# Two transformer blocks on one core: the overfull check moved up, low parts of weights split behind the first columns, and PE's unread products taken out of norms and routing and put at the start

## The reference, cut to what matters

```python
def reference(x, ...):                      # x: 256 tokens x 1024, float32
    x = first_block(x, ...)                 # 2 layers
    return second_block(x, ...)             # 2 layers

def first_block(...):
    h = x
    for i in range(2):
        mix = gla_mixer(h, ...) if i == 0 else mlstm_mixer(h, ...)
        h = layer_norm(ALPHA * h + mix, ln_g[i, 0], ln_b[i, 0])
        ffn = grouped_moe(h, router_w, moe_w1[i], moe_w3[i], moe_w2[i])
        h = layer_norm(ALPHA * h + ffn, ln_g[i, 1], ln_b[i, 1])
    return h

def grouped_moe(x, w_router, w1, w3, w2):   # 16 experts, 2 of them for each token
    aff = sigmoid(t @ w_router)             # the best group of 4 experts, the best 2 in it
    for e in range(16):
        y += gates[:, e:e + 1] * ((silu(t @ w1[e]) * (t @ w3[e])) @ w2[e])

def second_block(...):
    for l in range(2):
        h = rms(x, g_mix[l]) * (1.0 + sc1) + sh1
        parts = split(h @ w_in[l])          # attention over 256 keys and dilated attention
        ...
        x = x + gt1 * (mixed @ w_out[l])
        h2 = rms(x, g_mlp[l]) * (1.0 + sc2) + sh2
        x = x + gt2 * (square(relu(h2 @ w_ff1[l])) @ w_ff2[l])
```

## Time and profile before

| | us |
|---|---|
| median of three runs | 1489.74 |
| the profiled execution, its own time | 1487.12 |
| its span, first to last instruction | 1485.3 |
| PE busy | 1437.2 (97%) |
| PE weight loads busy | 1068.0 (72%) |
| DVE busy | 913.1 (61%) |
| ACT busy | 626.4 (42%) |
| POOL busy | 39.5 (3%) |

### The profile page before, as it was taken

The page is one execution under the profiler, slowest core; times in us unless marked ns, Lnnn a source line. Parts: engine busy times, 40 slices in busy tenths (PEclk is TensorE's granted clock), DMA queues, the critical chain, the costliest instruction groups (busy, mean ns, idle before and its releaser), DMA issues.

```text
span 1485.3 us, 20562 instructions
## 1 busy us (share of the span) xinstructions
PE 1437.2 (97%) x8426; PEld 1068.0 (72%) x8426; DVE 913.1 (61%) x1549; ACT 626.4 (42%) x1004; POOL 39.5 (3%) x39
## 2 busy tenths in 40 slices
PE   7999999989999999999799999999999999999998
PEld 7885444436888634443578997999977898899997
DVE  4986111117787711111799987998969976775555
ACT  6453211115344221211455655454456566465443
POOL 0000000000000000000120000000002000000000
PEclk9999999999999999999999999999999999999999
DMA  9897999998467899999565463899955533445540
GB/s 373 316 362 299 426 426 427 427 425 334 153 248 309 320 422 427 426 427 425 230 238 195 174 247 146 322 367 360 347 196 185 198 118 123 158 170 191 180 169 29
DMA packets 59063, 420.18 MB, mean 283 GB/s; under 512 B 6657, under 2 KB 6721, under 8 KB 8658
## 3 DMA queue, kind: packets, MB, share of 16 engines
q1 hardware_dynamic: 58322, 417.17, 71.3%
q0 software_dynamic: 640, 1.61, 0.3%
HBM read 417.71 MB, written 1.05 MB: 282 GB/s over the span
## 4 chain that ended last, share of the span: by engine, by line
PE 81%; DVE 11%; DMA 4%; ACT 3%; issue 1%; SPq 0%; DVEq 0%; ACTq 0%
PE ps L867 78%; DVE lo L2098 2%; DMA AR<-in_moe 2%; DMA raw<-in_moe 2%; DVE AR L2091 2%; PE ps L1505 1%; DVE AR L2088 1%; DVE TINY L2091 1%; ACT AR L1997 1%; PE ps L1476 1%; PE ps L1232 1%; DVE ACC L2091 0%; ACT T L1665 0%; PE ps L983 0%; DVE AR L2737 0%
## 5 line engine op out<-in xcount | busy, mean ns | idle before, releaser
L2098 DVE TENSOR_TENSOR lo<-raw,hi 128x1024 fp32r<-128x1024 f32 x296 | 359.7, 1239 | 96.5 <-ACT hi L1647 95.8
L1647 ACT ACTIVATE hi<-raw 128x1024 fp32r<-128x1024 f32 x296 | 306.0, 1056 | 182.5 <-PE ps L867 177.2
L867 PE MATMUL ps<-T,hi 128*128 128x256 f32 x1792 | 325.3, 284 | 8.4 <-ACT hi L1647 7.4
L867 PEld LDWEIGHTS ps<-T,hi 128*128 128x128 f32 x1792 | 278.6, 191 | 16.5 <-ACT hi L1647 7.4
L867 PE MATMUL ps<-hi,T 128*128 128x512 f32 x896 | 286.1, 394 | 3.5 <-ACT T L1665 3.2
L867 PE MATMUL ps<-T,lo 128*128 128x256 f32 x896 | 249.3, 281 | 0.0
L867 PEld LDWEIGHTS ps<-hi,T 128*128 128x128 f32 x896 | 168.2, 188 | 40.4 <-ACT T L1665 3.9
L867 PE MATMUL ps<-lo,T 128*128 128x512 f32 x448 | 174.5, 390 | 0.0
L867 PEld LDWEIGHTS ps<-T,lo 128*128 128x128 f32 x896 | 169.5, 190 | 0.0
L867 PE MATMUL ps<-hi,AF 128*128 128x512 f32 x512 | 163.3, 390 | 0.0
L2091 DVE SCALAR_TENSOR_TENSOR AR<-AR,ps 128x512 f32<-128x512 f32 x52 | 35.4, 685 | 189.4 <-PE ps L867 102.3
(11 more groups left out here) (247 smaller groups left out, 1730.7 us busy)
## 6 DMA issues: line engine op xcount, KB each, us to landing
raw<-in_moe SPq DMA_DIRECT2D x76, 1024.0 KB, 17.4
raw<-in_b_ff SPq DMA_DIRECT2D x64, 1024.0 KB, 5.0
AR<-in_moe SPq DMA_DIRECT2D x59, 1024.0 KB, 17.1
raw<-in_ada SPq DMA_DIRECT2D x48, 1024.0 KB, 6.6
ring<-in_moe SPq DMA_DIRECT2D x45, 1024.0 KB, 16.0
raw<-in_b_in SPq DMA_DIRECT2D x24, 1024.0 KB, 5.8
raw<-in_b_gate SPq DMA_DIRECT2D x16, 1024.0 KB, 4.7
ACC<-in_moe SPq DMA_DIRECT2D x12, 1024.0 KB, 20.3
```

The lines of the kernel that those rows point to most:

```text
L867: return e.matmul(o, l, r, start=a, stop=z, skip_group_check=True)
L1647: e.activation(hi[n % NC][:, :], raw[place[c]][:, 1024 * half:1024 * half + 1024], ACT.Copy).then_inc(*to("hi", "hi", n))
L2098: tt(lo[n % NC][:, :], r, hi[n % NC][:, :], SUB).then_inc(*to("lo", "lo", n))
```

## The change

It has four parts. (1) The check for overfull experts stands behind pair 7's second up product (s = 1, after the maps) in place of behind its first down product; SP's check stands 12 chunks from the layer's end in place of 6; the waits of the full computation name what is last there. (2) `turned_columns` hands out one low part behind the high part of columns 0 and one behind that of columns 2, for all norms; the single low parts ahead of the columns in `walk_ln` and `walk_rms`, and the one between `layer_norm(3)` and the first rms norm, are gone. In the first rms norm the gain is computed ahead of the scale. Where a first product used to wait for both parts of its unit, it now waits for the high one, and the products with the low part stand behind; the kernel's very first block is cut in two halves of four blocks of columns. (3) All `fill` calls in norms and routing are gone. (4) At the start PE runs 8 unread products on zeros that POOL has set.

```diff
-def turned_columns(kind, feed, late):
+def turned_columns(kind, feed):
     for g in range(4):
         yield (kind + "_turn", g)
         if g:
             yield (kind + "_split", g - 1)
         yield (kind + "_hi", g)
-        if g == 2:
-            yield from feed.some_late(late)
+        if g % 2 == 0:
+            yield from feed.some_late(1)
     yield (kind + "_split", 3)
...
     yield ("ln_rows",)
-    yield from feed.some_late(1)
-    yield from turned_columns("ln", feed, 1)
+    yield from turned_columns("ln", feed)
     yield from feed.some_late(NC)
...
     yield ("sum_up", key)
-    yield ("fill", 16)
     yield ("rows", 0, 0)
...
     yield ("x_lo", 0, 0)
-    yield ("fill", 5)
     yield ("places",)
...
         if p < 8 and s == (1 if p else 3):
             yield ("maps", p)
+        if p == 7 and s == 1:
+            yield ("overflow",)
...
-        if p == 7 and s == 4:
-            yield ("overflow",)
...
     yield from (("sum_turn", k) for k in sums)
+    if first:
+        yield ("rms_gain",)
     yield ("rms",)
     yield from (("sum_out", k) for k in sums)
-    yield ("rms_gain",)
-    yield from feed.some_late(1)
-    yield from turned_columns("rms", feed, 0)
+    if not first:
+        yield ("rms_gain",)
+    yield from turned_columns("rms", feed)
...
                     w.wait_ge(*after("hi", n0))
-                    for k in range(kt):
-                        if k % 2 == 0:
-                            w.wait_ge(*after(*xs[k // 2]))
-                        mm(o, hi[n0][:, 128 * k:128 * k + 128], th[:, k, :], k == 0, False)
-                        mm(o, hi[n0][:, 128 * k:128 * k + 128], tl[:, k, :], False, False)
-                    w.wait_ge(*after("lo", n0))
-                    for k in range(kt):
-                        ins = mm(o, lo[n0][:, 128 * k:128 * k + 128], th[:, k, :], False, k == kt - 1)
+                    for ks in (range(4), range(4, 8)):
+                        for k in ks:
+                            if k % 2 == 0:
+                                w.wait_ge(*after(*xs[k // 2]))
+                            mm(o, hi[n0][:, 128 * k:128 * k + 128], th[:, k, :], k == 0, False)
+                            mm(o, hi[n0][:, 128 * k:128 * k + 128], tl[:, k, :], False, False)
+                        w.wait_ge(*after("lo", n0))
+                        for k in ks:
+                            ins = mm(o, lo[n0][:, 128 * k:128 * k + 128], th[:, k, :], False, k == kt - 1)
...
                     w.wait_ge(*after(xs[0][0].replace("split", "hi"), *xs[0][1:]))
                     for t in range(2):
                         for k in range(2):
                             mm(PS[bank[name, 0, t]][:, :], th[:, k, 128 * t:128 * t + 128], h[:, HALF[k]], k == 0, False)
+                    w.wait_ge(*after("lo", n0))
+                    for t in range(2):
+                        for k in range(2):
                             mm(PS[bank[name, 0, t]][:, :], th[:, k, 128 * t:128 * t + 128], l[:, HALF[k]], False, False)
...
                     if what == "ln_turn":
-                        if a[0] == 0:
-                            fill(30)
                         turn_columns("ln", LN_XN, a[0], q)
...
+                p = take("fill")
+                w.wait_ge(*after("zeros"))
+                for _ in range(8):
+                    mm(p[0:64, 0:256], m.KM[:, 0, 0, 64:128], m.KM[:, 0, 0, 64:128].unsqueeze(1).broadcast_to([128, 4, 64]), True, True)
+                free.append(bank["fill",])
...
                     elif what == "rms_turn":
-                        if a[0] == 0 and blk == 2:
-                            fill(10)
-                        elif a[0] == 0 and l == 0:
-                            fill(24, ("x", 3, 0, 1))
                         turn_columns("rms", src, a[0], l, blk)
...
-            first_of = {c0 - 6: i for c0, i in stops.items()}
+            first_of = {c0 - 12: i for c0, i in stops.items()}
```

More of the change, by code:

```diff
@@ L669, in two_block_kernel @@
         XLO = sb("XLO", [128, 2, 1024], F32R)
+        XL1 = XLO[:, :, :].rearrange("p t d -> p (t d)")
         ACC = sb("ACC", [128, 2048])
@@ L940, in block_b @@
                 got = []
-                for u in us:
-                    got.append(unit(u))
                 if n == 0 and gs[0] == 0 and xs[0][0] in ("ln_split", "rms_split"):
-                    (h, l), = got
+                    n0 = plan.units[us[0]][2]
+                    h, l = hi[n0 % NC], lo[n0 % NC]
+                    w.wait_ge(*after("hi", n0))
                     w.wait_ge(*after(xs[0][0].replace("split", "hi"), *xs[0][1:]))
@@ L956, in block_b @@
                     return
+                for u in us:
+                    got.append(unit(u))
                 for t in range(2):
@@ L1014, in sum_turn @@
                 give(("sum_turn", key), "sum_out", key)
-            def fill(n, *ready):
-                p = take("fill")
-                for x in ready:
-                    w.wait_ge(*after(*x))
-                for _ in range(n):
-                    mm(p[:, 0:256], IDR[:, :], XLO[:, 0, 0:256], True, True)
-                free.append(bank["fill",])
             def layer_norm(q, turned):
@@ L1167, in moe @@
                         give(("logits", i), "logits_out", i)
-                    elif what == "fill":
-                        p = take("fill")
-                        for _ in range(a[0]):
-                            mm(p[:, 0:256], IDR[:, :], T2[:, 2048:2304], True, True)
-                        free.append(bank["fill",])
                     elif what == "count":
@@ L1286, in full_tensor @@
                 v.wait_ge(*after("f_x", i))
-                v.wait_ge(*after("turned", i, 7))
-                v.wait_ge(*after("y_lo", i, 6, 0))
+                v.wait_ge(*after("silu", i, 7))
+                v.wait_ge(*after("map", i, 7))
+                v.wait_ge(*after("gain", i, 7))
+                v.wait_ge(*after("y_lo", i, 5, 1))
+                v.wait_ge(*after("turned", i, 6))
                 for k in range(8):
@@ L1622, in tensor_program @@
             layer_norm(3, False)
-            feed.some_late(1)
             for l in range(2):
@@ L1856, in full_scalar @@
                 spare = [bank["spare", i, x] for x in range(4)] if not rehearsing[0] else range(4)
-                v.wait_ge(*after("down", i, 6, 0))
+                v.wait_ge(*after("up", i, 7, 0, 1))
                 for k in range(8):
@@ L2872, in vector_program @@
             layer_norm(3, False)
-            for what, *a in feed.some_late(1):
-                common(what, a)
             for l in range(2):
```

## The result

The changed kernel is slower by 0.27%: its time over that of the kernel before is 1.0027, with a 95% interval of 1.0019 to 1.0035. The medians of 13 runs each are 1493.3 and 1489.6 us. 1493.3 lies inside the forecast's wide range (1485.5 to 1495) and just outside the range of its likeliest case (1487 to 1493). The forecast had called "same within 0.2%" the likeliest, with 0.59; what came is "slower", which had 0.25.

A forecast was written before the change was run, and what follows sets the result against it. PE, with 81% of the chain, was taken as the bound through its idle time and clock, DMA second in moe. Terms summed to +1.0 us on 1487.1, so 1488.1, or 1490.2 on the timed level; range 1485.5 to 1495.

The forecast's parts named there:

- wide range: Whole kernel: range of the time over all cases, 1485.5 to 1495 us.
- likeliest case: Whole kernel: the forecast itself, 1490.2 us on the timed level, own range 1487 to 1493, chance 0.50.
- Start: Kernel's start: 8 products on zeros let the first real products run at full clock; -1.0 us (-1.4 to 0).
- Routing: Routing of both layers: without fills the clock falls for some 3.3 us; +1.0 each, +2.0 us (0 to +3.4).
- Check of layer 0: Layer 0's overflow check, moved earlier: DMA holds the next products back in turn; -0.2 us (-0.8 to 0).
- Check of layer 1: Layer 1's overflow check, moved earlier: PE catches up with DMA, last product starts sooner; -1.3 us (-1.5 to -0.8).
- `ln1`: Norm `ln1`: 4.8 us idle, transposes at half clock use up the new order's gain; +0.6 us (-1.0 to +2.7).
- First rms norm: First rms norm: cold transposes, but first product no longer held by gain and low part; -0.4 us (-1.3 to +1.7).
- The two rms norms: Rms norms ahead of feed forward: idle grows to about 2.6 us, clock may fall; +0.65 each, +1.3 us (0 to +3.4).
- Faster without any fall of the clock: Rival for routing and rms norms: without fills the clock doesn't fall; sum -3.9, 1485.3 us; chance 0.18.
- Slower, since the clock comes back only with real products: Rival at the norms: transposes don't raise the clock, first products run low; +5.9 more, 1496 us; chance 0.25.
- The start does nothing: Rival at the start: small load late or zero products run into 7.43; +1.0 more, 1491.2 us; chance 0.07.

The follow-up runs named there:

- experiment 5: Changed kernel with all unread products of norms and routing put back and the check, SP's too, in its old place; 1.0018 to the kernel before.
- experiment 2: Changed kernel with the unread products of routing alone put back (16 and 5 in each layer); 0.9989 to the kernel before.
- experiment 4: Kernel before with its unread products taken out and nothing else changed; 1.0052 to the kernel before, +7.7 us.
- experiment 6: Kernel before with the 8 products on zeros at the start added, nothing else changed; 1.0015 to the kernel before, slower by 2.2 us.
- experiment 7: Kernel before with only the low parts' new order; products, check and start as before; 0.9999 to the kernel before.
- experiment 10: Kernel before with 12 products on a constant added in `mlstm`, nothing else changed; 1.0002 to the kernel before.
- experiment 9: Changed kernel with 12 products on a constant added in a wait in `mlstm`, moving later code; 1.0016 to the kernel before.
- experiment 1: Changed kernel with all unread products of norms and routing put back, the rest of the change kept; 0.9980 to the kernel before.
- experiment 12: Changed kernel with all unread products put back, but the 24 ahead of the first rms norm as 24 transposes of a constant; 1485.1 us (one run).
- experiment 3: Changed kernel with the unread products of the norms alone put back (30, 24, 10 and 10); 1.0001 to the kernel before.
- experiment 8: Changed kernel with 4 in place of 8 products at the start, 16 PE instructions fewer; 1497.8 us (one run).

## Why the prediction was right or wrong, step by step

The wide range held the time, and the bounding reasons were right: PE's waits and its clock set the time, the products lay in idle time, and what they did was to hold the clock. The likeliest case came out wrong by the sizes of its losses, and by one wait that it didn't have.

**Start: right in this execution.** -1.0 forecast, -0.98 in the ledger. In two of the other nine traces with products at the start the clock fell at 20 us and took 2.2 and 3.5 us back (experiments 5 and 2). And the same 8 products also moved all later code of PE by 32 instructions, which no step of the prediction looked at.

**Routing: mechanism right, size wrong.** Forecast +1.0 a layer "for a stretch like the 3.3 us of 701.20 to 704.50". Measured +1.8 and +2.2, with the clock low for 6.8 us in each. The one stretch that I had was taken for the length of them all; the other in the earlier trace rows, 6.7 us, would have given the right size.

**Check of layer 0: -0.2 forecast, -0.5 in the ledger, more in most executions.** Here the profiled execution of the kernel before misled me. It is the only one of six kernels with the check in the old place whose clock did not fall there (it did in experiments 4, 5, 6, 7 and 10). That the medians differ by 2 us less than the two profiles fits a fall of this kind in most executions of the kernel before. The mean granted clocks bear it out: the profiled execution has 0.997, and of the 78 timed beside the experiments 64 have 0.992 to 0.995. One more stretch of 6.8 us at 0.50 in 1485 makes 0.997 into 0.994. The 64 have a median of 1489.4 us and the other 14 one of 1488.0. So the forecast was made from one of the few lucky executions; where the clock fell in the others is not on record.

**Check of layer 1: wrong in its result.** Forecast -1.3, measured -0.1. The earlier check did what was hoped for: 1.49 us idle, no fall of the clock. In experiment 9, which has no second wait, the difference to the kernel before is +4.0 us at the end of routing and +1.8 behind the check, a gain of 2.2. The second wait of 2.79 us took it back. What the earlier place gives is a shorter idle time: in all 14 checks of the seven other kernels that have it there, and in both of the changed kernel, it was 1.3 to 1.8 us, against 2.3 to 3.6 in the 12 of the six kernels with the old place. In 11 of these 12 the clock fell, at the check or, in two, behind the second wait. Why it is shorter is seen in the loads of PE's code, in the last section.

**`ln1`: size wrong.** Forecast +0.6, if the clock was back soon after 350. The first product came at 350.66, as forecast (350.8), but the clock came back only at 353.4 and took the rest: +1.5. The sign that the forecast named for this (0.50 for over 5 us behind the transposes) came only if it is counted from their start: 6.1 us, against 2.4 from their end. And of the order's gain, for which the bounds had 1.0, experiments 1 and 7 show 0.3 left at the block's end, as the low part is then waited for.

**First rms norm: right**, -0.4 forecast, -0.6 measured together with `ln3`. The clock was low for 13.7 us, of which only 6 had work.

**The two rms norms: half right.** Forecast +0.65 each; measured +0.4 with 3.4 us at 0.50, and +2.0 with 6.8. As with routing, the length of the stretch decides.

**The rivals.** *Faster without any fall of the clock* is excluded by the windows. *Slower, since the clock comes back only with real products* named the side that came, for a reason that did not: experiment 12 has it back during transposes, and `ln1` and the first rms norm did not lose over 2 us each against the forecast. The Trainium skill, "TensorE: Matmul & The Clock Gate", Part 4 (PE-mode transpose), has it that the full clock doesn't engage for transposes. For getting it back the trace of experiment 12 disagrees: 0.50 until 723.4, 1.00 behind it, and no product from the first transpose (720.58) to 728.74. For keeping it the traces are divided. The forecast had one stretch of transposes alone at 1.00, from 1106.5 to 1111.7. In 11 of the 14 traces it is so; in three (experiments 3, 8 and 10), none of which changes anything there, the clock fell in it, as in experiment 3:

```profile
1110.63 3.01 PE L999 MATMUL ps<-cst,AR 128*128 128x128 f32 x16 [1.35 <-DVE AR L2095]
```

*The start does nothing* is excluded by its own place, but on the whole it came out worse than that when added alone (experiment 6, of whose loss the part at layer 1's check is explained).

The sum of the parts by the ledger is -1.0 + 4.0 - 0.5 - 0.1 + 1.5 - 0.6 + 2.4 = +5.7, against the forecast's +1.0. Of the 4.7 between them, clock stretches longer than reckoned make 2.0 in routing, 0.9 in `ln1` and 1.1 in the rms norms, and code that was not loaded 1.2 at the check of layer 1. The small differences at layer 0's check and the first rms norm (-0.5) make the rest. That the measured time came only 3.1 us over the forecast's 1490.2, and so inside the wide range, is in part luck: the loss of 5.7 us between the two profiles is 3.7 between the medians, and that the profile of before was a lucky one the forecast didn't know.

## What to carry to other kernels

Unread products in a wait are not idle work if they hold the clock: ask of each wait what the clock does behind it without them, and price a fall by several stretches at 0.50 in the trace, not by the shortest. A change that adds or removes PE's instructions moves all code behind them; if the program branches over a long block, look in both traces for a second wait for issue behind the branch before believing a difference of a few microseconds: one in the middle of a product, with a packet of code moving in it. And compare the profiled execution's mean granted clock with that of the timed ones: where it is higher (0.997 against 0.994 here), the profile lacks a fall that its like mostly have, and two profiles differ by more than the kernels do.

## What the runs showed of the hardware that was not expected

PE meets code that is not loaded behind a branch. In the 2.6 us of the second wait, and of the wait at the kernel before's check, one packet of the instruction queue q8 moves. I take q8 for PE's: in the kernel before it moves 70 packets, and PE has 16,852 products and weight loads, the other engines together some 2,600 instructions. From one restart of PE to the next it is 5.3 to 5.8 us, however much PE worked between: 10 records and 2.79 us idle, 18 and 1.10, 12 and 2.47, 1 and 5.21. The queues (packets, MB, share) of the changed kernel from 693.6 to 696.2, and behind them those of the kernel before from 697.5 to 700.1:

```profile
q1 hardware_dynamic: 143, 1.04, 98.9%
q8 instruction: 1, 0.02, 2.6%
q14 instruction: 1, 0.01, 0.8%
```
```profile
q1 hardware_dynamic: 155, 1.11, 102.0%
q8 instruction: 1, 0.02, 2.1%
```

The starts of q8's packets in the 14 traces show how the waits are made. At all 28 checks PE restarts 1.5 to 1.7 us behind the end of the last packet. At the check's new place that packet starts 0.7 to 1.2 us before PE goes idle, at the old one between 0.2 us before and 0.4 behind: hence the shorter idle time. The next packet starts 2.8 to 3.5 us behind the restart, also where nobody waits for it (686.31 and 691.95 in experiment 3, 688.24 and 693.90 in experiment 9). So a second wait comes only where PE gets to the end of the loaded code before that packet is there. Why the packet starts earlier at the new place isn't shown.

The data queue is full all the while (98.9% and 102.0%), and that may be why one such packet takes so long to come; no run had the branch with quiet queues, so this stays open. In a stretch of straight code the packets are not waited for: from 150 to 240 us of the kernel before, with 446 records of PE, there are these of the two instruction queues:

```profile
q8 instruction: 4, 0.07, 0.3%
q14 instruction: 2, 0.02, 0.0%
```

The Trainium skill, "Advanced Engine Details and Errata", ISA Cache, has the code in lines of 16 KB or 256 instructions. The trace agrees: 446 products with their weight loads are 892 instructions, 3.5 such lines, and 4 packets of q8 moved; over the whole kernel 16,852 make 65.8 lines, and 70 packets moved.

Where the second wait falls followed the count of instructions ahead in four kernels (a record is one product with its weight load, two instructions; a float32 product has two records): 10 records behind the branch in the changed kernel, 18 with 8 records fewer ahead, 12 with the start's 16 records added to the kernel before, and 16 with 12 added to it, which means 28 in the kernel before itself, where no wait is seen.
